# One-hot tiles made once, parked in DRAM and loaded back for the second layer of an expert mixer

## What is computed

```python
q = (xc @ wq).reshape(PEER_CHUNK, PEER_HEADS, 2, PEER_QDIM // 2)
sc = jnp.einsum('thpd,pkd->thpk', q, subkeys)
sv, si = lax.top_k(sc, PEER_TOPK)
...                                   # 16 of the 256 pairs per head: key numbers i1, i2
e = i1 * PEER_NKEYS + i2
g = jax.nn.softmax(cv.astype(jnp.float32), axis=-1)
act = jax.nn.gelu(jnp.einsum('td,thkd->thk', xc, u[e]))
return jnp.einsum('thk,thkd->td', g * act, v[e])
```

## Time and profile before

| | |
|---|---|
| median of 3 runs | 1138.44 us (1137.85 to 1139.14) |
| the profiled execution | 1137.64 us, of which span 1135.8 us |
| PE / DVE / ACT / POOL busy share of the span | 97% / 76% / 65% / 22% |
| DMA, mean | 160 GB/s, 16 engines busy 48% of the span |
| TensorE's granted clock | 0.997 of full speed |

### The profile page before, as it was taken

The page is one execution under the profiler, slowest core; times in us unless marked ns, Lnnn a source line. Parts: engine busy times, 40 slices in busy tenths (PEclk is TensorE's granted clock), DMA queues, the critical chain, the costliest instruction groups (busy, mean ns, idle before and its releaser), DMA issues.

```text
span 1135.8 us, 22485 instructions
## 1 busy us (share of the span) xinstructions
PE 1097.2 (97%) x7174; PEld 978.7 (86%) x7174; DVE 858.5 (76%) x1701; ACT 739.9 (65%) x1426; POOL 245.7 (22%) x196
## 2 busy tenths in 40 slices
PE   6999999998999999999999999999999999999998
PEld 5788888798999999999999999977777777888887
DVE  5755666675899998989888888889999996444444
ACT  4345556664344444458888888899999997454553
POOL 0000222100000112640000000034334343545553
PEclk9999999998999999999999999999999999999999
DMA  7464222264445555554444444444444445556563
GB/s 252 149 235 141 80 84 75 89 197 160 159 140 182 172 183 185 185 172 162 148 148 148 148 148 148 149 142 156 150 164 148 155 159 190 199 187 200 186 197 115
DMA packets 50016, 181.34 MB, mean 160 GB/s; under 512 B 5552, under 2 KB 5680, under 8 KB 49968
## 3 DMA queue, kind: packets, MB, share of 16 engines
q1 hardware_dynamic: 49968, 180.72, 48.2%
HBM read 178.60 MB, written 2.10 MB: 159 GB/s over the span
## 4 chain that ended last, share of the span: by engine, by line
PE 87%; DVE 7%; ACT 2%; issue 2%; DMA 1%; POOL 0%; SPq 0%; DVEq 0%; POOLq 0%; ACTq 0%
PE bank L679 30%; PE bank L628 9%; PE bank L629 9%; PE bank L630 9%; PE bank L642 6%; PE bank L322 4%; PE bank L323 3%; PE bank L324 3%; DVE lo L1302 2%; PE bank L571 1%; DMA raw<-wpre_d 1%; PE bank L336 1%; PE bank L338 1%; PE bank L337 1%; PE bank L382 1%
## 5 line engine op out<-in xcount | busy, mean ns | idle before, releaser
L1302 DVE TENSOR_TENSOR lo<-raw,hi 128x1024 fp32r<-128x1024 f32 x253 | 315.6, 1252 | 152.2 <-ACT hi L925 147.7
L925 ACT ACTIVATE hi<-raw 128x1024 fp32r<-128x1024 f32 x253 | 268.0, 1060 | 223.9 <-PE bank L630 125.7
L628 PE MATMUL bank<-xhi,hi 128*128 128x256 f32 x1024 | 293.8, 287 | 0.8 <-DVE lo L1302 0.8
L629 PE MATMUL bank<-xlo,hi 128*128 128x256 f32 x1024 | 289.6, 283 | 0.0
L630 PE MATMUL bank<-xhi,lo 128*128 128x256 f32 x1024 | 289.4, 283 | 0.0
L1532 POOL TENSOR_TENSOR auxl<-big,auxh 128x256 fp32r<-128x256 f32 x128 | 174.5, 1364 | 452.7 <-ACT auxh L951 452.7
L628 PEld LDWEIGHTS bank<-xhi,hi 128*128 128x128 f32 x1024 | 196.2, 192 | 2.2 <-issue 1.1
L629 PEld LDWEIGHTS bank<-xlo,hi 128*128 128x128 f32 x1024 | 196.4, 192 | 0.0
L630 PEld LDWEIGHTS bank<-xhi,lo 128*128 128x128 f32 x1024 | 196.1, 192 | 0.0
L942 ACT ACTIVATE oneB<-kep,eT 128x128 fp32r<-128x128 f32 x512 | 162.2, 388 | 0.0
L679 PE MATMUL bank<-hi,auxh 128*128 128x512 f32 x508 | 160.7, 398 | 1.3 <-ACT hi L925 1.0
(11 more groups left out here) (233 smaller groups left out, 1588.2 us busy)
## 6 DMA issues: line engine op xcount, KB each, us to landing
raw<-u_d SPq DMA_DIRECT2D x128, 512.0 KB, 3.3
raw<-v_d SPq DMA_DIRECT2D x128, 512.0 KB, 3.2
raw<-wpre_d SPq DMA_DIRECT2D x78, 512.0 KB, 4.0
big<-x_d SPq DMA_DIRECT2D x2, 512.0 KB, 3.7
out_d<-big SPq DMA_DIRECT2D x2, 512.0 KB, 5.2
big<-out_d SPq DMA_DIRECT2D x2, 512.0 KB, 5.1
out_d<-big SPq DMA_DIRECT2D x4, 256.0 KB, 2.1
big<-cst_d SPq DMA_DIRECT2D x1, 719.5 KB, 8.6
```

Of the source, the lines that this page charges most:

```text
L628: pe.matmul(out, wh, xhi[:, k, :], start=(k == 0), stop=False)
L629: pe.matmul(out, wh, xlo[:, k, :], start=False, stop=False)
L925: act.activation(hi[:, n % SPLIT, :], raw[:, n % RING, :], ACT.Copy).then_inc(hi_done, 1)
L1302: dve.tensor_tensor(lo[:, n % SPLIT, :], raw[:, n % RING, :], hi[:, n % SPLIT, :].bitcast(F32), ALU.subtract).then_inc(lo_done, 1)
```

## The change

The one-hot `oneB` is made only for the 64 groups of the lower half. GpSimd subtracts the picked numbers from 0..127 for all four tokens at once (`distances`, 128 x 512), ScalarE squares the result in one activation and applies the Relu in a second (`fold_b`). `oneB` gets three buffers (SLOTS) in place of two. SyncE stores each finished `oneB` (256 KB) to DRAM scratch `ob_d`, in its queue ahead of a u tile's load; in the v stage it loads each back into its slot, ahead of a v tile's load, once the group three before has been multiplied. `same` goes from two buffers to one, so `keys_equal` runs for the group two ahead, not three. The weights move from `eT` to `gsum`.

```diff
-            stream(u_d, N_PRE, 0, NBLK)
-            stream(v_d, N_PRE + NBLK, 0, HALF)
+            def fetch(src, first, at_, i, j):
+                sp.wait_ge(lo_done, i * UNROLL + splits(first + at_ + j - RING + 1))
+                load((first + at_ + j) % RING,
+                     src[bass.ds(i * UNROLL + (at_ + j), 1)].rearrange("a p c -> (a p) c"))
+            def save_b(i, j, base):
+                g = base + j
+                sp.wait_ge(S("oneB_ready"), i * UNROLL + (g + 1))
+                sp.dma_start(ob_d[bass.ds(i * UNROLL + g, 1)].rearrange("a p c -> (a p) c"),
+                             oneB[:, g % SLOTS, :, :].rearrange("p t k -> p (t k)").bitcast(F32)
+                             ).then_inc(ob_saved[g % SLOTS], 16)
+            def load_b(i, j, base):
+                g = base + j
+                sp.wait_ge(S("g_ready"), i * UNROLL + (NGRP + g - SLOTS + 1))
+                sp.dma_start(oneB[:, g % SLOTS, :, :].rearrange("p t k -> p (t k)").bitcast(F32),
+                             ob_d[bass.ds(i * UNROLL + g, 1)].rearrange("a p c -> (a p) c")
+                             ).then_inc(ob_in[g % SLOTS], 16)
+            def fetch_and_save(i, j):
+                save_b(i, j, 1)
+                fetch(u_d, N_PRE, HALF + LEAD, i, j)
+            def fetch_and_load(i, j):
+                load_b(i, j, 3)
+                fetch(v_d, N_PRE + NBLK, LEAD, i, j)
+            stream(u_d, N_PRE, 0, HALF + LEAD)
+            save_b(0, 0, 0)
+            each_tile(sp, HALF - LEAD, fetch_and_save)
+            for j in range(LEAD - 1):
+                save_b(0, j, HALF - LEAD + 1)
+                fetch(v_d, N_PRE + NBLK, 0, 0, j)
+            fetch(v_d, N_PRE + NBLK, 0, 0, LEAD - 1)
+            for q in range(SLOTS):
+                sp.wait_ge(ob_saved[q], 16 * len(range(q, NGRP, SLOTS)))
+            for g in range(SLOTS):
+                load_b(0, g, 0)
+            each_tile(sp, HALF - LEAD, fetch_and_load)
+            for j in range(HALF - LEAD + SLOTS, NGRP):
+                load_b(0, 0, j)
...
-                pe.wait_ge(S("oneB_ready"), i * UNROLL + (g + 1))
+                if g < NGRP:
+                    pe.wait_ge(S("oneB_ready"), i * UNROLL + (g + 1))
+                else:
+                    pe.wait_ge(ob_in[(g - NGRP) % SLOTS], i * (16 * UNROLL // SLOTS) + 16 * ((g - NGRP) // SLOTS + 1))
...
-            def one_hot_b(i, j, base):
+            def fold_b(i, j, base):
                 g = base + j
-                if g >= 2:
-                    act.wait_ge(S("g_ready"), i * UNROLL + (g - 1))
-                B = oneB[:, g % 2, :, :].bitcast(F32)
-                for t in range(4):
-                    i2 = eT[:, 1, bass.ds(i * (4 * UNROLL) + (4 * (g % NGRP) + t), 1)]
-                    m = act.activation(oneB[:, g % 2, t, :], iota, ACT.Square, bias=i2, scale=-1.0)
-                m.then_inc(S("dist_sq"), 1)
+                B = oneB[:, g % SLOTS, :, :].bitcast(F32)
+                act.wait_ge(S("dist"), i * UNROLL + (g + 1))
+                act.activation(oneB[:, g % SLOTS, :, :], B, ACT.Square).then_inc(S("dist_sq"), 1)
                 act.wait_ge(S("dist_sq"), i * UNROLL + (g + 1))
-                act.activation(oneB[:, g % 2, :, :], B, ACT.Relu, bias=1.0,
+                act.activation(oneB[:, g % SLOTS, :, :], B, ACT.Relu, bias=1.0,
                                scale=-1.0).then_inc(S("oneB_ready"), 1)
...
-                one_hot_b(i, j, NGRP + 2)
                 loop_hi(i, V0 + j + SPLIT)
                 w_hi(i, j + SPLIT)
...
-                    keys_equal(i, j, base + 3)
+                    keys_equal(i, j, base + 2)
                 weigh(i, j, base)
...
+            def distances(i, j, base):
+                g = base + j
+                if g >= SLOTS:
+                    pool.wait_ge(S("g_ready"), i * UNROLL + (g - SLOTS + 1))
+                    pool.wait_ge(ob_saved[g % SLOTS], i * (16 * UNROLL // SLOTS) + 16 * (g // SLOTS))
+                i2 = eT[:, 1, bass.ds(i * (4 * UNROLL) + 4 * g, 4)].unsqueeze(2).broadcast_to([P, 4, P])
+                pool.tensor_tensor(oneB[:, g % SLOTS, :, :], iota.unsqueeze(1).broadcast_to([P, 4, P]), i2,
+                                   ALU.subtract).then_inc(S("dist"), 1)
+            pool.wait_ge(S("bank67_read"), 2)
+            for g in range(SLOTS):
+                distances(0, g, 0)
+            each_tile(pool, NGRP - SLOTS, lambda i, j: distances(i, j, SLOTS))
```

More of the change, by code:

```diff
@@ L61 @@
 SPLIT = 3
+SLOTS = 3
+LEAD = 7
 UNROLL = 12
@@ L109, in build @@
         kep = sb("kep", [P, NKEP])
-        eT = sb("eT", [P, 3, T])
+        eT = sb("eT", [P, 2, T])
         gw2 = sb("gw2", [P, T, 2], F32R)
-        same = sb("same", [P, 2, 4, HALF])
+        same = sb("same", [P, 4, HALF])
         oneA = sb("oneA", [P, 2, 4, 2, HALF], F32R)
         gsum = sb("gsum", [P, HALF, 4])
-        oneB = sb("oneB", [P, 2, 4, P], F32R)
+        gw_ = gsum[:, :, :].rearrange("p e t -> p (e t)")
+        oneB = sb("oneB", [P, SLOTS, 4, P], F32R)
+        ob_d = nc.dram_tensor("ob_d", (NGRP, P, 4 * P), F32, kind="Internal").ap()
         flatA, flatB = (oneA[:, :, :, :, :].rearrange("p q t r k -> p (q t r k)"),
-                        oneB[:, :, :, :].rearrange("p q t k -> p (q t k)"))
+                        oneB[:, 0:2, :, :].rearrange("p q t k -> p (q t k)"))
         ohi = (flatB.rearrange("p (k t) -> p k t", k=4), xhi[:, 4:8, :])
@@ L201, in build @@
         kep_in = sem("kep_in")
+        ob_saved = [sem(f"ob_saved{q}") for q in range(SLOTS)]
+        ob_in = [sem(f"ob_in{q}") for q in range(SLOTS)]
         hi_done = sem("hi_done")
@@ L636, in g_group @@
                 pe.wait_ge(S("oneA_ready"), i * UNROLL + (g + 1))
-                pe.wait_ge(S("oneB_ready"), i * UNROLL + (g + 1))
+                if g < NGRP:
+                    pe.wait_ge(S("oneB_ready"), i * UNROLL + (g + 1))
+                else:
+                    pe.wait_ge(ob_in[(g - NGRP) % SLOTS], i * (16 * UNROLL // SLOTS) + 16 * ((g - NGRP) // SLOTS + 1))
+                slot = g % NGRP % SLOTS
                 pe.wait_ge(S("bank67_read"), i * UNROLL + (g + 1))
                 for t in range(4):
-                    m = pe.matmul(bank[6 + g % 2][:, 2 * t * HALF:2 * (t + 1) * HALF], oneB[:, g % 2, t, :],
+                    m = pe.matmul(bank[6 + g % 2][:, 2 * t * HALF:2 * (t + 1) * HALF], oneB[:, slot, t, :],
                                   oneA[:, g % 2, t, :, :], start=True, stop=True)
@@ L958, in u_step_g @@
             def u_step_g(i, j):
-                one_hot_b(i, j, 1)
+                fold_b(i, j, 1)
                 loop_hi(i, N_PRE + HALF + j + SPLIT)
@@ L972, in _ @@
             act.wait_ge(S("bank67_read"), 2)
-            act.activation(gw2[:, :, 0], eT[:, 2, :], ACT.Copy).then_inc(S("gw2_hi"), 1)
-            one_hot_b(0, 0, 0)
+            act.activation(gw2[:, :, 0], gw_, ACT.Copy).then_inc(S("gw2_hi"), 1)
+            fold_b(0, 0, 0)
             for j in range(ROUTER, HALF):
@@ L977, in _ @@
             each_tile(act, HALF - 1, u_step_g)
-            one_hot_b(0, 0, NGRP)
             act.wait_ge(S("weighed"), 1 + NGRP)
@@ L1400, in _ @@
             dve.tensor_copy(eT[:, 0:2, :], bank[6][:, :].rearrange("p (w t) -> p w t", w=2)).then_inc(S("bank67_read"), 1)
-            dve.tensor_copy(eT[:, 2, :], bank[7][:, 0:T]).then_inc(S("bank67_read"), 1)
+            dve.tensor_copy(gw_, bank[7][:, 0:T]).then_inc(S("bank67_read"), 1)
             dve.wait_ge(S("bank67_read"), 2)
@@ L1410, in keys_equal @@
                 e0 = 0 if g < NGRP else HALF
-                if g >= 2:
-                    dve.wait_ge(S("oneA_ready"), i * UNROLL + (g - 1))
+                if g >= 1:
+                    dve.wait_ge(S("oneA_ready"), i * UNROLL + g)
                 i1 = eT[:, 0, bass.ds(i * (4 * UNROLL) + 4 * (g % NGRP), 4)].unsqueeze(2).broadcast_to([P, 4, HALF])
-                dve.tensor_tensor(same[:, g % 2, :, :], iota[:, e0:e0 + HALF].unsqueeze(1).broadcast_to([P, 4, HALF]),
+                dve.tensor_tensor(same[:, :, :], iota[:, e0:e0 + HALF].unsqueeze(1).broadcast_to([P, 4, HALF]),
                                   i1, ALU.is_equal).then_inc(S("same"), 1)
@@ L1420, in rows_a @@
                 dve.wait_ge(S("same"), i * UNROLL + (g + 1))
-                eq_ = same[:, g % 2, :, :].unsqueeze(2).broadcast_to([P, 4, 2, HALF])
+                eq_ = same[:, :, :].unsqueeze(2).broadcast_to([P, 4, 2, HALF])
                 w_ = gw2[:, bass.ds(i * (4 * UNROLL) + 4 * (g % NGRP), 4), :].bitcast(F32)
@@ L1442, in _ @@
             dve.wait_ge(S("gw2_hi"), 1)
[L1443 to L1448, removed]
+            link(dve.tensor_tensor(gw2[:, :, 1], gw_, gw2[:, :, 0].bitcast(F32), ALU.subtract))
+            for g in range(2):
+                keys_equal(0, g, 0)
+                rows_a(0, g, 0)
             for j in range(ROUTER, HALF):
@@ L1451, in _ @@
             dve.wait_ge(S("bank45_read"), NH + HALF // 2)
```

(4 more changed lines are left out.)

2 lines of the change are left out of this document (removed).

## The result

The changed kernel takes 1167.93 us against 1138.76 us: ratio 1.0262, 95% interval 1.0248 to 1.0276, slower by 29 us. I had forecast slower by 18 us (1156.7), a ratio of 1.016, with a range that ends at 1168, which is 1.026 of the time before: the result lies at the very edge of that range, and 11 us are missing from my sum. Its profiled execution has a span of 1166.5 us, 30.7 more than before.

What follows compares the result with a forecast made beforehand. PE, waiting for ScalarE, was taken as today's bound, and VectorE, held by GpSimd's port, as the u stage's next. 17 - 5 + 1.5 + 4.5 = +18.3 on 1138.4 gave 1156.7 us, own range 1148 to 1166, overall 1134 to 1168.

Steps and rivals of the forecast that it cites:

- What bounds the kernel, and that ScalarE's relief is worth nothing in the u stage: Both stages: PE waits for ScalarE; once relieved, VectorE bounds the u stage, so ScalarE's 0.64 us per tile gains nothing.
- The u stage, +17: Groups GpSimd makes in its loop: steps of 4.04 and 3.6, mean 3.82 against 3.53, +0.28 for each of 61.
- GpSimd's port as the cause, the arrival as the price: u stage: GpSimd's subtraction blocks VectorE's SBUF reads; loss 0.46 behind `lo`, up to 1.05 us by its arrival.
- The rival in which the store is early: u stage: store saved before the next `lo` ends, subtraction queues behind `lo`, step 3.50; 1136.6 us, chance 0.20.
- The start, +1.5: Before group 0: three subtractions (3.6 us) alternate with VectorE's first `same` and `oneA`; +1.5 us (0 to 3).
- The seam, +4.5: Between the stages: group 64's load stands behind a v tile's load, 6.4 us until it may run; +4.5 (3 to 6).
- The v stage, -5: v-stage groups: the landing of `oneB` loads sets intervals of 3.31 against 3.395, over 62 tiles; -5 us (-12 to +5).
- "`w_lo` falls behind `lo` as now": v stage: GpSimd's `w_lo` keeps its place behind `lo`, beside VectorE's reduction; no cost of its own given.

Runs made afterwards that it cites:

- e2: The changed kernel with one more wait: GpSimd's subtraction starts only when VectorE has finished `oneA` of the group before; 1137.42 us.
- e1: The changed kernel with GpSimd subtracting four numbers in place of 128 x 512 from group 3 on, values wrong; 1136.9 us.
- e3: The changed kernel with each store reading another tile of the same size and the subtraction not waiting for the store, values wrong; 1137.64 us.
- e10: The changed kernel with `w_lo` of v tiles 3 to 63 waiting for VectorE's `oneA`, nothing else altered; 1166.02 us.
- e9: The kernel of e8 with `w_lo` of v tiles 3 to 63 waiting until VectorE has finished `oneA` of that step; 1116.24 us, ratio 0.9818.
- e12: The kernel of e9 with the first three `oneB` loaded behind the last v tile's load again, as in the changed kernel; 1123.75 us.
- e6: The changed kernel with `oneB` slots numbered on through both halves, first three loads ahead of the last v tile's load, later loads a step earlier; 1168.52 us.
- e7: The kernel of e6 with ScalarE's four squares as before the change in place of GpSimd's subtraction; 1143.63 us, three runs at 1143 to 1145, one at 1128.
- e8: The kernel of e2 with the slot numbering and the earlier `oneB` loads of e6; 1137.37 us.
- e11: The kernel of e7 with the wait of e9 on `w_lo`; 1126.49 us, all four runs within 1125 to 1129.

## Why the prediction came out as it did

- **What bounds the kernel, and that ScalarE's relief is worth nothing in the u stage:** right. PE waits for `oneA` where it waited for the Relu.
- **The u stage, +17:** measured +16.9, which is luck: groups 10 to 62 give +16.7, groups 4 to 10 -1.3, and the first four steps +1.9, of the slow clock and of group 3's late `oneB`, both of which I had at nothing. Nor are the steps as I had them. I had the store landing at E + 4.0; it lands at E + 4.8 (E, the end of `lo`, is 604.15 + 1.21 - 3.85 = 601.51; the store issued at 602.29 lands 4.0 later, at 606.3), since SyncE issues it 0.6 us behind the load and not 0.4, and it takes 4.0 and not 3.6 from there. I had steps of 3.6 and 4.04 in turn; there is one phase, in the weighing, with 0.83 lost and not 1.05. Behind `lo` the subtraction costs 0.25 (e2) and not 0.46: it takes 1.04 alone, not 1.2, and lets the path go before its recorded end (`same` ends 0.28 after it in e2, and takes 0.41 alone). Forecast was +0.28 a step, measured +0.32: the errors went both ways and cancelled.
- **GpSimd's port as the cause, the arrival as the price:** right, by e1, e2 and e3. e2's 30 us for one wait is the strongest of them. The Trainium skill's rule in SBUF — State Buffer, Who interferes with whom (the loser blocks for the whole instruction) gives the mechanism. The changed kernel's trace agrees: `oneA` ends only 0.54 after the subtraction's end. e2 shows that only 0.25 of a 1.04 us operation is left to pay when it starts behind `lo`.
- **The rival in which the store is early:** its mechanism is real, its price was wrong. I gave it 1136.6 by steps of 3.50 and gains elsewhere; e2 and e3 are there (1137) by steps of 3.31 and with the seam's losses.
- **The start, +1.5:** measured +1.6 up to group 0, and 1.9 more in the first four steps behind it (0.8 in the first, at the lower clock: 0.71 from 515 to 520; 1.2 in the third, waiting for the first subtraction that stands behind a store). I had priced the wait ahead of group 0 and neither of these.
- **The seam, +4.5, is the first step that failed:** +11.3 up to group 70. Of my 6.4 us from the end of the last u tile to group 64 the chain `hi`, `lo`, load, `load_b` is there as I put it (759.36 to 765.70 is 6.3), but it begins 1.8 after that tile's end (757.54), since ScalarE waits for VectorE's weighing of group 63 (ending at 759.0); I had given that 1 us. Two terms were missing, put at nothing without a reason. After 8 us of idle TensorE's clock is at 0.50, 2.3 us for group 64 and its tile. And the load for group 68 stands in SyncE's queue behind the tile load that waits for the next `lo` (774.22 to 775.43), whose `hi` waited in turn for PE to finish that slow first tile (771.39): issued at 776.20, 2.36 of idle for PE, and 1.65 more for group 68 and its tile at a slow clock (4.86 in place of 3.21).
- **The v stage, -5, is the second:** the steady part, groups 70 to 127, came to 3.398 on the mean and not 3.31. My landing was right on the median (S + 2.6 + 0.59 + 3.4 = S + 6.6; I had 6.57), and the median interval is 3.30. But I took the median for the mean. In these groups a load takes 3.2 to 5.2 us to land, 3.5 on the mean, and its issue slips too, in a few steps to S + 3.6 or later; an early one gains nothing, because PE's own 3.21 holds, and a late one is paid in full (the load that took 5.2 made an interval of 4.99). 29 of the 57 groups start within 0.1 us of their load's landing. 57 x 0.09 = 5 us. e10 shows that `w_lo` has no part in it, e9 and e12 that with loads a step ahead and `w_lo` placed it is 3.21.
- **"`w_lo` falls behind `lo` as now":** true in the changed kernel's steady v stage, but it hung on something that I had not named. In e6, e7 and e8, where PE no longer waits for loads, `w_lo` falls elsewhere and costs 0.32 us a step. That VectorE's wait for `hi` kept it in place fits the rows, but no run tests it by itself; that its place is the cause, e9 and e11 show.

## What to carry to other kernels

Where two engines share a path, price an operation by when it arrives, not by its length: the same 1.04 us cost 0.83 or 0.25 a step, and a wait that places it was worth 30 us. A phase (the place in the step at which an operation arrives) that is right because somebody else is late can go wrong when that wait is mended; fix it with a wait of its own before judging the mend. A transfer whose median lands at its deadline is late half the time: ask for it a step earlier. And where a change makes TensorE wait between two stages, leave room in the sum for the slow clock behind the wait.

## What the runs showed that I had not expected

A stall costs TensorE more than its length: after 8.16 us of idle the granted clock was 0.50 for about 5 us more, which made 3.2 us of work 5.49 long; it fell again around the 2.36 us of idle soon after, and at the start, around 1.90 us of idle. Early in the changed kernel's u stage (groups 3 to 10) the intervals were 3.31 to 3.39 with the full subtraction in place, until the landing of the stores settled in the weighing at 3.85: the same instructions fit two phases. e7's one run at 1128 beside three at 1144 looks like two phases of `w_lo`, as with its place fixed (e11) all four runs are at 1125 to 1129; but the run at 1128 has no trace, so that stays open. The stores and loads of 256 KB beside 512 KB for every tile, 237 to 250 GB/s with the 16 engines busy 73 to 81%, left PE without a gap in e9: bytes alone cost no time here.
